# One state-space chunk's lead-in reordered in a hybrid decoder block: decay rows first, gating on VectorE, first norm, turn and projection one iteration earlier

## The reference, cut to what matters

```python
def ssd_chunked(x, dt, a, bm, cm):           # 8 chunks of 128 tokens, 8 heads of 64
    a_cs = jnp.cumsum(adt, axis=-1)
    decay = jnp.exp(segsum(adt))
    cb = jnp.einsum('bclgn,bcsgn->bcgls', cc, bc)
    y_diag = jnp.einsum('bcgrls,bcsgrp->bclgrp', cb[:, :, :, None] * decay, xd)
    states = jnp.einsum('bclgn,bcgrl,bclgrp->bcgrpn', bc, decay_states, xd)
    ...                                       # state carried from chunk to chunk
    y_off = jnp.einsum('bclgn,bcgrpn,bcgrl->bclgrp', cc, prev, jnp.exp(a_cs))
    return (y_diag + y_off).reshape(b, s, h, p)

y_ssd = ssd_chunked(xs, dt, a, bs, cs) + d_skip * xs
y_ssd = rms_norm(y_ssd * jax.nn.silu(z), ssd_norm)
y_mla = rms_norm(y_mla, mla_out_norm)
y = jnp.concatenate([y_ssd, y_mla], axis=-1) @ w_out
x = x + g1 * rms_norm(y, post_norm_mix)       # then norm, router, experts
```

## Time and profile before

| | before |
|---|---|
| median of 3 runs | 981.52 us (978.11 to 982.55) |
| profiled execution, device time | 980.25 us |
| profiled execution, span of the trace | 978.5 us |
| mean granted TensorE clock | 0.99 |
| TensorE busy (matrix products) | 944.4 us, 97% of the span |
| VectorE, ScalarE, GpSimd busy | 513.8, 309.2, 220.8 us |
| the stage begins, first projection, first iteration with `t` >= 0 | 441.6, 469.0, 485.4 us |

### The profile page before, as it was taken

How to read it: one execution, slowest core, us unless ns; L and a number is a source line. 1 busy time by engine, 2 the same in 40 slices (tenths; PEclk the granted TensorE clock), 3 DMA queues, 4 the chain that set the end, 5 groups by cost and what they waited for, 6 DMA issues and landing times.

```text
span 978.5 us, 15190 instructions
## 1 busy us (share of the span) xinstructions
PE 944.4 (97%) x5431; PEld 565.2 (58%) x5431; DVE 513.8 (53%) x933; ACT 309.2 (32%) x622; POOL 220.8 (23%) x270
## 2 busy tenths in 40 slices
PE   7999999999989999999999999989999999999986
PEld 6544444444546667668666665575555555555562
DVE  2266447444765656565678885573333333333337
ACT  3130002222544444432233232143333333333313
POOL 2110001122700670002344422012222222222003
PEclk9999999999999999998999999999999999999998
DMA  9996525000000000006023327978999999999657
GB/s 324 358 326 218 214 113 139 2 1 0 7 0 1 1 1 1 2 1 239 21 87 111 105 87 299 362 280 309 390 414 407 403 409 400 407 415 414 242 221 307
DMA packets 56370, 196.66 MB, mean 201 GB/s; under 512 B 15603, under 2 KB 27003, under 8 KB 40803
## 3 DMA queue, kind: packets, MB, share of 16 engines
q1 hardware_dynamic: 48180, 178.39, 48.0%
q0 software_dynamic: 6816, 17.18, 4.6%
q10 hardware_dynamic: 1296, 0.07, 0.1%
HBM read 178.27 MB, written 24.69 MB: 207 GB/s over the span
## 4 chain that ended last, share of the span: by engine, by line
PE 49%; DVE 3%; issue 1%; ACT 1%; ACTq 0%; POOL 0%; DVEq 0%
PE PS L1704 16%; PE PS L1572 12%; PE PS L1730 9%; PE PS L1678 2%; PE PS L1483 2%; PE PS L1594 1%; PE PS L1539 1%; PE PS L1761 1%; PE PS L1713 1%; PE PS L1555 1%; PE PS L1584 1%; DVE y_sum L2352 1%; DVE y_sum L2359 1%; PE PS L1528 1%; PE PS L1520 1%
## 5 line engine op out<-in xcount | busy, mean ns | idle before, releaser
L1704 PE MATMUL PS<-ring,xg_T 128*64 x736 | 162.7, 379 | 0.8 <-ACT xg_T L1865 0.8
L1704 PE MATMUL PS<-near_gu,xg_T 128*64 128x256 f32 x736 | 162.7, 379 | 0.0
L1704 PEld LDWEIGHTS PS<-ring,xg_T 128*64 128x64 f32 x736 | 100.7, 137 | 60.0 <-issue 13.4
L1572 PE MATMUL PS<-w_out_sb,cat_T 128*128 128x512 f32 x256 | 117.0, 602 | 2.2 <-DVE y_sc L2047 1.9
L1025 PE MATMUL PS<-hT,w_x 128*128 128x512 f32 x256 | 112.1, 594 | 0.0
L448 POOL TENSOR_SCALAR rstd<-stat 128x1 f32<-128x1 f32 (+1 forms) x48 | 21.4, 447 | 351.8 <-ACT junk L631 174.5
L1704 PEld LDWEIGHTS PS<-near_gu,xg_T 128*64 128x64 f32 x736 | 100.7, 137 | 0.0
L1730 PE MATMUL PS<-ring,hid_T 128*64 x184 | 83.8, 598 | 0.4 <-DVE hid_T L2294 0.4
L1730 PE MATMUL PS<-near_dn,hid_T 128*64 128x512 f32 x184 | 83.9, 598 | 0.0
L1025 PEld LDWEIGHTS PS<-hT,w_x 128*128 128x128 f32 x256 | 47.8, 190 | 58.5 <-issue 58.2
L2285 DVE TENSOR_TENSOR hid<-PS,hid_s 128x128 f32<-128x128 f32 x46 | 11.2, 286 | 129.8 <-PE PS L1704 129.8
(11 more groups left out here) (348 smaller groups left out, 1556.4 us busy)
## 6 DMA issues: line engine op xcount, KB each, us to landing
ring<-in_w_gate_dram SPq DMA_DIRECT2D x32, 1024.0 KB, 11.5
ring<-in_w_up_dram SPq DMA_DIRECT2D x32, 1024.0 KB, 13.8
ring<-in_w_down_dram SPq DMA_DIRECT2D x32, 1024.0 KB, 15.9
ada_later<-in_ada_w_dram SPq DMA_DIRECT2D x16, 1024.0 KB, 4.8
ada_first<-in_ada_w_dram SPq DMA_DIRECT2D x16, 512.0 KB, 9.4
y_g<-y_rows SPq DMA_DIRECT2D x8, 1024.0 KB, 12.8
x_in<-in_x_dram SPq DMA_DIRECT2D x8, 512.0 KB, 7.9
w_out_sb<-in_w_out_dram SPq DMA_DIRECT2D x1, 4096.0 KB, 13.1
```

The costliest lines, as they stand in the source:

```text
L1572: last = pe.matmul(BANK[out_bank(t) + j], cat_T[t % 2][:, k, :], w_out_sb[:, k, j * HALF:(j + 1) * HALF], start=(k == 0), stop=(k == KC - 1))
L1704: last = pe.matmul(BANK[2 + s_][rows_, 0:FF], xg_T[b][:, k, rows_], gu[u][:, s_, k, :], start=(k == 0), stop=(k == KC - 1))
```

## The change

It concerns iterations -3, -2 and -1 only.

- TensorE, start of the stage: the decay rows of chunk 0, both groups, are issued at once, before the turns of chunk 0, into banks 2 and 3. The router's small product goes behind the turns, and its addition on VectorE to the end of iteration -3.
- VectorE, iteration -3: both `arg_of(0, ...)` come ahead of `xd_of(0)`. Iteration -2: `y_diag(0)` adds the skip term straight out of the bank and then multiplies by the gate, all on VectorE; GpSimd's `gated_y(0)` is gone. `joined(0)` moves ahead of `arg_of(1, 1)`, and `cat_half(0)` moves from iteration -1 to the end of `masked(1, 1)` in iteration -2.
- ScalarE: the square over `y_mla` of tile 0 is taken in iteration -3, ahead of the two exponentials; the square over the gated part in iteration -2 right behind `b_of(1)`, and `cat_half(0)` follows in the same iteration.
- GpSimd, iteration -2: `inverse_root` of tile 0 comes ahead of `decayed(1)`.
- TensorE, iterations -2 and -1: 12 fillers are left of 32 (8 ahead of `diagonal(0)`, 4 ahead of the first projection). `cat_T_of(0)`, then `states(1)`, the 4 fillers and the first 8 products of `project(0)` stand at the end of iteration -2. Iteration -1 is then `diagonal(1)`, `turned(2)`, `cat_T_of(1)` and the rest of `project(0)`.

```diff
@@ gpsimd
-                    if tile(t + 2):
+                    if t == -2:
+                        inverse_root(pool, 3, 0, S["y_sq_done"], 2, 2, "rstd_y")
+                        decayed(1)
+                    elif tile(t + 2):
                         gated_y(t + 2)
-                    if tile(t + 3) and t + 3 < NT - 1:
+                    if tile(t + 3) and t + 3 < NT - 1 and t != -2:
                         decayed(t + 3)
-                    if tile(t + 2):
+                    if tile(t + 2) and t != -2:
                         inverse_root(pool, 3, t + 2, S["y_sq_done"], 2 * (t + 3), 2, "rstd_y")
@@ tensor
+                def first_rows_of(g):
+                    for j in range(HG):
+                        h = g * HG + j
+                        last = pe.matmul(BANK[2 + g][:, j * P:(j + 1) * P], adt[:, 0, h:h + 1].to_broadcast([P, P]),
+                                         tri[:, :], start=True, stop=True)
+                    last.then_inc(S["ssd_rows"], 1)
...
-                pe.wait_ge(S["fold_pool"], 1)
-                pe.matmul(BANK[5][:, 0:NG + E], ones[:, :], fold_r[:, 0, :], start=True, stop=True).then_inc(S["fold_pe"], 1)
+                first_rows_of(0)
+                first_rows_of(1)
...
                 for t in range(-3, NT):
-                    if t == -2 or t == -1:
-                        busy(7, 6)
+                    if t == -2:
+                        pe.wait_ge(S["cums_read"], 2)
+                        busy(7, 8)
                     if tile(t + 2):
                         diagonal(t + 2)
-                    if t == -1:
-                        busy(7, 4)
                     if tile(t + 3):
                         turned(t + 3)
                         decay_rows(t + 3, 0)
-                    if t == -2:
-                        busy(7, 7)
-                    if t == -1:
-                        cat_T_of(0)
-                        busy(7, 4)
-                        pe.wait_ge(S["w_out_loaded"], 16)
+                    if t == -3:
+                        pe.wait_ge(S["fold_pool"], 1)
+                        pe.matmul(BANK[5][:, 0:NG + E], ones[:, :], fold_r[:, 0, :], start=True, stop=True).then_inc(S["fold_pe"], 1)
                     if 1 <= t < NT - 1:
                         route(t - 1)
-                    if tile(t + 1):
+                    if tile(t + 1) and t >= 0:
                         project(t + 1, 0, 4)
...
-                    if t == -3:
-                        pe.wait_ge(S["cums_read"], 2)
-                        busy(7, 5)
                     if tile(t + 3):
                         decay_rows(t + 3, 1)
-                    if tile(t + 1):
+                    if t == -2:
+                        cat_T_of(0)
+                        states(1)
+                        busy(7, 4)
+                        pe.wait_ge(S["w_out_loaded"], 16)
+                        project(0, 0, 8)
+                    if tile(t + 1) and t >= 0:
                         project(t + 1, 4, 8)
                     if tile(t + 2) and t >= -1:
                         cat_T_of(t + 2)
@@ scalar
+                def first_squares():
+                    act.wait_ge(S["ssd_y"], 1)
+                    act.wait_ge(S["y_sq_done"], 1)
+                    act.activation(junk[:, 0:IN_SSD], zs[:, 0, :], ACT.Square, scale=IN_SSD ** -0.5,
+                                   accum_out=stat[:, 3, 0:1]).then_inc(S["y_sq_done"], 1)
@@ vector, y_diag
-                        ins = dve.tensor_tensor(y, BANK[3], y, ALU.add)
-                    else:
-                        ins = dve.tensor_copy(y, BANK[3])
-                    ins.then_inc(S["ssd_y1"], 1)
+                        dve.tensor_tensor(y, BANK[3], y, ALU.add).then_inc(S["ssd_y1"], 1)
+                        return
+                    dve.wait_ge(S["ssd_xsk"], 1)
+                    dve.tensor_tensor(y, BANK[3], xsk[0][:, :], ALU.add).then_inc(S["ssd_ysum"], 1)
+                    dve.wait_ge(S["ssd_ysum"], 1)
+                    dve.sem_inc(S["ssd_y1"], 1)
+                    dve.tensor_tensor(zs[:, 0, :], y, zs[:, 0, :], ALU.mult).then_inc(S["ssd_y"], 1)
```

More of the change, by code:

```diff
@@ L1488, in decay_rows @@
                 def decay_rows(ch, g):
-                    if ch >= PE_ROWS:
+                    if not 0 < ch < PE_ROWS:
                         return
-                    if ch or g:
-                        pe.wait_ge(S["ssd_arg"], 2 * ch + g)
+                    pe.wait_ge(S["ssd_arg"], 2 * ch + g)
                     for j in range(HG):
@@ L1631, in _ @@
                         project(t + 1, 8, 12)
-                    if tile(t + 3):
+                    if tile(t + 3) and t != -2:
                         states(t + 3)
@@ L1830, in _ @@
                         b_of(t + 3)
-                    if t == -1:
-                        cat_half(0)
+                    if t == -2:
+                        first_squares()
                     if tile(t + 2) and t >= -1:
@@ L1836, in _ @@
                         x2_square(t)
+                    if t == -3:
+                        act.activation(junk[:, 0:INNER], y_mla[:, 0, :], ACT.Square, scale=INNER ** -0.5,
+                                       accum_out=stat[:, 4, 0:1]).then_inc(S["y_sq_done"], 1)
                     if tile(t + 3):
@@ L1840, in _ @@
                     if t == -2:
-                        y_squares(0)
+                        cat_half(0)
                     if tile(t + 2) and t >= -1:
@@ L1957, in _, with folded @@
                 dve.tensor_copy(acs_T[:, :], BANK[4][0:NH, 0:P]).then_inc(S["cums_read"], 1)
-                dve.wait_ge(S["fold_pe"], 1)
-                dve.tensor_tensor(rb_row[:, :], BANK[5][:, 0:NG + E], rb_row[:, :], ALU.add).then_inc(S["fold_dve"], 1)
+                def folded():
+                    dve.wait_ge(S["fold_pe"], 1)
+                    dve.tensor_tensor(rb_row[:, :], BANK[5][:, 0:NG + E], rb_row[:, :], ALU.add).then_inc(S["fold_dve"], 1)
                 def xd_of(ch):
@@ L1985, in arg_of @@
                         dve.wait_ge(S[f"rows_here{ch % 2}"], 16 * (ch // 2))
-                    spread = BANK[2] if ch < PE_ROWS else d
+                    spread = BANK[2 + g * (ch == 0)] if ch < PE_ROWS else d
                     link(dve.tensor_tensor(d.rearrange("p (h l) -> p h l", l=P), spread.rearrange("p (h l) -> p h l", l=P),
@@ L2129, in _ @@
                         y_diag(t + 2)
+                    if t == -3:
+                        arg_of(0, 0)
+                        arg_of(0, 1)
                     if tile(t + 3):
                         xd_of(t + 3)
-                    if t == -1:
-                        cat_half(0)
                     if t == NT - 1:
@@ L2146, in _ @@
                     if tile(t + 3):
-                        arg_of(t + 3, 0)
+                        if t > -3:
+                            arg_of(t + 3, 0)
                         cb_of(t + 3)
                         xsk_of(t + 3)
+                    if t == -2:
+                        joined(0)
                     if tile(t + 2) and t >= -1:
@@ L2157, in _ @@
                     if tile(t + 3):
-                        arg_of(t + 3, 1)
+                        if t > -3:
+                            arg_of(t + 3, 1)
                         masked(t + 3, 0)
@@ L2167, in _ @@
                         state_of(t + 3)
-                    if t == -2:
-                        joined(0)
+                    if t == -3:
+                        folded()
                     if t == -1:
```

## The result

The changed kernel takes 989.29 us (median of 4 executions, 986.2 to 993.7) against 981.34 us before: ratio 1.0093, 95% interval 1.007 to 1.0116. It is slower by 8 us. The two intervals overlap between 1.007 and 1.0085. The profiled execution took 987.03 us with a span of 985.2 us, 6.7 us more than the one of before. The prediction's own sum was 986.3.

What follows compares the result with a forecast made beforehand. TensorE was taken as the bound, the lead-in's handover moving the end one for one. Terms 0.0 + 3.8 + 2.3 = +6.1 us on the profiled 980.25 gave 986.3 us; range 980 to 990.

Steps and rivals of the forecast that it cites:

- The prediction's own sum: Whole kernel: +6.1 us on the profiled execution's 980.25 us, giving 986.3 us.
- term 1: Iteration -3: the reordering leaves the start of chunk 0's diagonal unmoved, 0.0 us, bounds -1.0 and +1.0.
- term 2: Iteration -1: turns of tile 1 wait for tile 1's norm and start later, +3.8 us, bounds +3.0 and +4.2.
- term 3: Behind the wait ahead of tile 1's turns: clock at half for 3.5 to 6.0 us, costing +2.3 (1.7 to 3.0).
- the norm of tile 1 lost its cover: Iteration -1: turns of tile 1 wait for its whole norm, which before lay beside fillers, tile 0's turns and 6.94 us of projection.
- 9.63 us: Iteration -1, chunk 1's diagonal to the end of tile 1's join: 1.93 to the emptying plus 7.70 to the join.
- The wait was to be 6.6 us: Iteration -1: TensorE idle about 6.6 us, from 473.1, ahead of the turns of tile 1.
- the first projection starts 5.85 us earlier: End of iteration -2: tile 0's first projection starts at 463.15 us instead of 469.00.
- a start after 465: Sign of being wrong: first projection starting after 465 us, then +2 us more.
- the join of tile 0: Iteration -2, VectorE: joined(0), behind cb and xsk, ends near 459.5 us.
- the clock also falls in iteration -2: Rival: clock falls among holes of 1.3, 1.4 and 0.6 us, another 1.7 us or more, 988 to 990; chance 0.10.
- takes 0.57 alone: Iteration -2, VectorE: the argument's second operation, stretched by GpSimd in the trace before, takes 0.57 us alone.

Runs made afterwards that it cites:

- e1: Changed kernel with 17 fillers put back in iterations -3 and -2; 987.85 us, ratio 1.0063 to the kernel before.
- e2: Changed kernel with 28 fillers inside TensorE's wait ahead of the turns of tile 1; 985.22 us, ratio 1.0057 to the kernel before.
- e3: Changed kernel with both the 17 fillers of e1 and the 28 of e2; 985.68 us, ratio 1.0057 to the kernel before.
- e10: The changed kernel executed again, nothing edited, on another chip; 987.09 us, ratio 1.0064 to the kernel before.
- e4: Changed kernel with the first eight products of tile 0's projection and their four fillers' place back behind turned(2), those fillers dropped; 978.85 us, ratio 0.999.
- e11: Changed kernel with the projection back behind turned(2), 1 instead of 8 fillers ahead of diagonal(0), none of the 17 fillers of e9; 976.95 us, ratio 0.9964.
- e6: Kernel before with chunk 0's decay rows first, in banks 2 and 3, and their arguments ahead of xd(0); 981.2 us, ratio 1.0009.
- e7: Kernel before with chunk 0's skip term and gate on VectorE alone, GpSimd's operations for it gone; 979.02 us, ratio 0.9998.
- e9: e4 with the 17 fillers of e1, and 1 instead of 8 fillers ahead of diagonal(0); 977.3 us, ratio 0.9972 to the kernel before.
- e8: Kernel before without 21 of its 32 fillers, nothing else changed; 982.23 us, ratio 1.0022.

## Why the prediction was right or wrong

The prediction's terms, measured in the two profiles of the changed kernel against the profile of before (us, from the table above). "Clock held" is the 28.07 us that e1, e2 and e3 all have from diagonal(0) to the turns of tile 1 (28.06 to 28.08), against 23.50 before:

| | forecast | changed | e10 |
|---|---|---|---|
| term 1, diagonal(0) | 0.0 | -0.44 | +0.22 |
| term 2, diagonal(0) to turns of tile 1, clock held | +3.8 | +4.57 | +4.57 |
| half clock in iteration -2 | nothing | +2.80 | +1.34 |
| term 3, behind the wait | +2.3 | +1.70 | +2.64 |
| tile 1's projection | +6.1 | +8.63 | +8.77 |

**What held.** The mechanism was the forecast one: the norm of tile 1 lost its cover. From diagonal to join and turns I had added 9.63 us from two rows; 9.68 to 9.71 were measured in the changed kernel, e1, e2, e3 and e10. The wait was to be 6.6 us and is 6.68. Moving the eight products back removes the loss (e4). Term 1 is within its bounds of 1.0 in every profile of this order; what it is in an execution goes with when the clock returns at the stage's start. Term 3 was +2.3 (1.7 to 3.0); the stretch from the turns to tile 1's projection, 14.16 us with the clock held, took 15.74 in the changed kernel, 16.39 in e1 and 16.68 in e10: 1.6, 2.2 and 2.5 us, the first just under the lower bound. The Trainium skill (TensorE: Matmul & The Clock Gate, part 1) has the idle gap bring back the throttled state. The profiles of the changed kernel, e1 and e10 agree: each has the clock at 0.50 behind its 6.68 us wait.

**What failed: iteration -2.** The step that failed is "the first projection starts 5.85 us earlier", at 463.15 us, 10.5 behind diagonal(0). It came 11.5 behind it with the clock held (e1, e2, e3), 12.86 in e10 and 14.32 in the changed profile. In us from the start of the span it came at 467.31 in the changed profile and at 466.64 in e10, or 466.3 and 465.5 without the stage's later start. The prediction had named a start after 465 as a sign of being wrong, with 2 us more to pay. Two things were put at nothing in this step, and the bounds of term 2, 3.0 to 4.2, had no room for either.

The first is the join of tile 0, which is in every profile of this order. It was to end at 459.5, 6.9 us behind diagonal(0). It ends 7.84 behind:

```profile
459.31 1.23 POOL L1413 TENSOR_TENSOR state_d<-state,slim 128x512 f32<-128x512 f32 x1
459.57 1.26 DVE L2055 TENSOR_SCALAR cat<-y_mla,rstd 128x512 f32<-128x512 f32 x1
```

The second scaling takes 1.26 us beside GpSimd's `carried(1)` (L1413, which scales the state for chunk 1), and 0.47 without it (L2055 at 483.33 in the same profile): 0.8 of the 0.9 us. The prediction had looked at what GpSimd does beside the new gating on VectorE, but not at what it does beside the moved join. Mostly by this, term 2 is +4.6 with the clock held, above its upper bound.

The second is the clock. The rival "the clock also falls in iteration -2" was given 0.10 and left out of the sum, with the argument that every hole there is shorter than the 1.56 us that had left the clock alone at 489 us. The holes were read right: 1.28 and 1.55 us in the timeline. The inference from one hole was wrong. At 489 us a single hole stands behind 3.0 us of narrow products and ahead of 7.1 us of long ones. Here two holes, and one of 1.88 us ahead of the state products, stand among narrow turns and rows; at 457 to 461 us TensorE was busy for 0.00, 0.83, 0.33 and 0.12 of successive microseconds. Of the five profiles with these holes open, the changed kernel, e10 and e11 fell there and e2 and e4 did not. Of the six in which fillers stand in iteration -2 (before, e1, e3, e6, e7 and e9) none fell; e8, with a hole of 1.75 us there and 1.55 and 1.01 behind it, fell at 465.9. This makes it likely that open holes bring the fall, and doesn't prove it: what decides in a given execution stays open. The hole ahead of the state products was 1.88 to 1.96 us in the three that fell and 1.43 in the two that didn't, but no run varied it by itself.

The trace of before had a warning: at 597.9 us the clock fell with TensorE counted 0.70 busy in that microsecond, behind narrow products and a wait of only 0.30 us. I had seen it only as a chance event and didn't use it.

**What the times say.** The price of 2.80 and 1.34 us is read from two profiles. The medians don't show it: e1 against e10 and e3 against e2, which differ in the 17 fillers, have the same ratios. Nor do they settle the 1.7 to 2.6 us of term 3: e2, without the fall behind the wait, has 1.0057 and e10, with it, 1.0064, and their intervals overlap. With medians, the changed kernel is +8.0 us on its before (interval 6.9 to 11.4) and in e10 +6.7 on its 980.35; the forecast was +6.1. So how much of the miss in the first measurement is this clock, in executions that were not profiled, isn't known, nor why the two medians differ.

**The sum's base.** 986.3 was made on the profiled execution of 980.25; the profiled execution after took 987.03. That this is so near is luck: the lead-in cost 8.6 us and the stage began 1.0 later, and two later half-clock stretches of before are missing. The median of 989.29 contains executions up to 993.7.

**Two small readings.** The argument's second operation "takes 0.57 alone" was read from a row that itself lies beside GpSimd's `xds` (447.81 to 448.85); with GpSimd idle it takes 0.43 (451.11 us in the same trace). The start of rows (1, 1) comes out as forecast all the same. The clock's return before was at 447.7, not 447.6.

**The parts.** The gate on VectorE gives a ratio of 0.9998 by itself and rows first 1.0009: neither brings or costs what can be told. In its one profile, e6 has diagonal(0) 1.45 us later, with the clock's return 0.5 us later as a part of it. e4, with the turns and the join of tile 0 an iteration earlier and its projection where it was, has 0.999, which can't be told from no change. e9 and e11 are faster than before; they also have 1 filler instead of 8 ahead of diagonal(0), and which of the two makes them faster was not tried. In the profiles, diagonal(0) is 1.8 us sooner in e9 than in e4 (9.71 against 11.50), and from there to the turns of tile 1 both take 21.4 us.

## What to carry to other kernels

In a pipeline written out by hand, a long piece of work that is hoisted also delays what stands behind it; look first at what it covered where it stood. Here eight products moved ahead of the diagonal took the cover off a 9.7 us chain over four engines, and the same eight behind it cost nothing. When an operation moves, look also at what runs beside it on other engines in its new place: it cost 0.8 us here. And that one hole of 1.56 us left the clock alone did not mean that several such holes among narrow products would: three profiles of five had a fall there, at 1.3 and 2.8 us in the two that were priced. Give such a fall a term of its own, and don't count on the medians to show it: those of e1 and e10 did not.

## What the runs showed of the hardware

- The clock returned between 3.6 and 6.9 us behind the stage's first product (3.6 in e11, 3.7 in the changed profile, 6.1 before, 6.9 in e8), with the same or nearly the same stream of products from the start. Between e3 and e1, which have the same order up to there, it goes with 1.1 us at diagonal(0) (10.41 and 11.53; the clock back at 3.6 and 6.7).
- Half-clock stretches of 3.4 us appear in some executions of an order and not in others: near 289 us in the changed kernel, e1, e2, e3, e4 and e9, not in the others; between 595 and 611 us in before, e1, e3, e9 and e10, not in the others. In 35 executions of the kernel before, the times were 976.9 to 985.0 us and the mean granted clocks 0.998 to 0.988. The four at 0.988 took 982.5 us and more.
- VectorE beside GpSimd: the scaling of `cat`, 128x512 f32, took 1.26 us where GpSimd's multiplication ran beside it (L2055 at 459.57 us, changed profile) and 0.47 without (L2055 at 483.33).
